# A projection stage rewritten: unrolled, with the vector work of one head pair laid behind the products of the next

## What is computed

```
def token_shift_mix(z, mu):
    prev = jnp.pad(z[:, :-1], ((0, 0), (1, 0), (0, 0)))
    nxt = jnp.pad(z[:, 1:], ((0, 0), (0, 1), (0, 0)))
    return z + mu * (0.5 * (prev + nxt) - z)

def rwkv_prepare(zs, w0, w2, a0, a2, g2, k_k, k_a):
    ...
    r, k, v, wd, ad, gd = [zs[..., bounds[i]:bounds[i + 1]] for i in range(6)]
    ...
    w_log = -jax.nn.softplus(-(w0 + jnp.einsum('btdl,dlc->btdc', jnp.tanh(wd), w2))) - 0.5
    decay = jnp.exp(-jnp.exp(w_log.astype(jnp.float32)))
    iclr = jax.nn.sigmoid(a0 + jnp.einsum('btdl,dlc->btdc', ad, a2))
    gate = jax.nn.sigmoid(gd) @ g2
    kk = split_heads(k * k_k).astype(jnp.float32)
    kk = kk * lax.rsqrt(jnp.maximum(jnp.sum(kk * kk, axis=-1, keepdims=True), L2_EPS * L2_EPS))
    k_dir = k[:, :, None, :] * (1.0 + (iclr - 1.0) * k_a)
```

## Time and profile before

| | |
|---|---|
| median of 3 runs | 2924.93 us (2923.62 to 2926.19) |
| the profiled execution, its own time | 2919.25 us |
| its span, first to last instruction | 2917.6 us |
| mean granted TensorE clock | 0.883 |
| busy in the span | TensorE 2215.9 us, VectorE 1730.8, ScalarE 859.6, GpSimd 721.5 |
| instructions | 41,994 |

### The profile page before, as it was taken

One profiled execution on the slowest core, in us unless ns is written; L12 is line 12 of the kernel. 1 busy time (PEld: TensorE's weight loads), 2 busy tenths in 40 slices (PEclk: granted clock), 3 DMA queues, 4 the chain that ended last, 5 costly groups with the idle time before them and its releaser, 6 DMA issues. The chain is left out here.

```text
span 2917.6 us, 41994 instructions
## 1 busy us (share of the span) xinstructions
PE 2215.9 (76%) x16681; PEld 1386.4 (48%) x16681; DVE 1730.8 (59%) x3472; ACT 859.6 (29%) x1718; POOL 721.5 (25%) x607
## 2 busy tenths in 40 slices
PE   5667667398767688887888898878777777777876
PEld 2645545187642677876665454333333332333332
DVE  2367767642582033433556666877777777777764
ACT  4244444232442323332332222222122212221221
POOL 0000000080000111111004333444444444444441
PEclk8888888699768699998999999999999999999898
DMA  3222322342523433230539999999999999999995
GB/s 159 69 88 86 148 109 86 143 150 81 225 99 124 176 140 133 90 140 17 187 128 399 363 384 342 421 411 420 421 420 420 421 421 420 420 421 421 421 421 220
DMA packets 119316, 741.36 MB, mean 254 GB/s; under 512 B 16065, under 2 KB 23265, under 8 KB 48353
## 3 DMA queue, kind: packets, MB, share of 16 engines
q0 software_dynamic: 73728, 536.90, 44.7%
q1 hardware_dynamic: 44256, 199.88, 18.5%
q10 hardware_dynamic: 1152, 2.10, 0.2%
HBM read 683.14 MB, written 55.69 MB: 253 GB/s over the span
## 5 line engine op out<-in xcount | busy, mean ns | idle before, releaser
L2278 PE MATMUL bank<-uv,dg 128*128 128x512 f32 x1664 | 810.4, 644 | 232.3 <-ACT dg L2086 227.4
L2278 PEld LDWEIGHTS bank<-uv,dg 128*128 128x128 f32 x1664 | 333.7, 205 | 699.6 <-issue 408.9
L2171 DVE SCALAR_TENSOR_TENSOR junk<-uv,gr 128x1024 f32<-128x1024 f32 x416 | 509.9, 1226 | 219.1 <-DMA uv<-in_uv_in,ic 193.3
L2009 POOL DMA_INDIRECT uv<-in_uv_in,ic x416 | 461.0, 1108 | 663.3 <-PE bank L2278 584.7
L2081 ACT ACTIVATE ge<-dt_ 128x4 f32<-128x4 f32 x128 | 26.5, 207 | 927.5 <-DVE junk L2171 927.4
L91 PE MATMUL bank<-ht_hi,wh 128*128 128x256 f32 (+1 forms) x432 | 164.4, 381 | 110.0 <-DVE wl L477 73.9
L2278 PE MATMUL bank<-uvx,dg 128*128 128x512 f32 x384 | 190.3, 653 | 56.5 <-ACT dg L2086 56.5
L2086 ACT ACTIVATE dg<-ident,gc_ 128x128 f32<-128x128 f32 x512 | 164.2, 392 | 29.4 <-DVE gc_ L2177 29.2
L91 PEld LDWEIGHTS bank<-ht_hi,wh 128*128 128x128 f32 x432 | 96.0, 222 | 136.3 <-issue 102.2
L92 PE MATMUL bank<-ht_lo,wh 128*128 128x256 f32 (+1 forms) x432 | 158.5, 367 | 0.0
L2278 PEld LDWEIGHTS bank<-uvx,dg 128*128 128x128 f32 x384 | 78.1, 209 | 168.7 <-issue 92.3
(11 more groups left out here) (357 smaller groups left out, 3982.9 us busy)
## 6 DMA issues: line engine op xcount, KB each, us to landing
pair_record<-rec SPq DMA_DIRECT2D x8, 4364.0 KB
wm<-in_wmod SPq DMA_DIRECT2D x16, 1024.0 KB, 5.1
wraw<-in_wpair_in SPq DMA_DIRECT2D x8, 1536.0 KB, 14.9
ab<-pair_record SPq DMA_DIRECT2D x16, 768.0 KB, 6.3
wz<-in_wz_in SPq DMA_DIRECT2D x20, 512.0 KB, 3.5
wm<-in_wmod SPq DMA_DIRECT2D x4, 2048.0 KB, 21.4
wraw<-in_wq_in SPq DMA_DIRECT2D x16, 512.0 KB
uv<-in_uv_in,ic POOLq DMA_INDIRECT x416
```

What stands on the lines that cost most here:

```text
L2009: pool.indirect_dma_start(ring(i), None, g["uv_in"], bass.IndirectOffsetOnAxis(ap=ic[:, s % ICR, k:k + 1], axis=0)).then_inc(su[row_slot[i ...
L2171: dve.scalar_tensor_tensor(junk[:, :], ring(i)[:, 0:D], 1.0, hc[:, t % 2, :], ALU.mult, ALU.mult, accum_out=dt[:, k:k + 1]).then_inc(s_ud, 1)
L2278: mm = pe.matmul(acc(t, c)[:, :], dg[:, n % 2, k, :], ring(i)[:, D + 512 * c:D + 512 * c + 512], start=h == 0 and q == 0 and k == 0, stop= ...
```

## The change

`project` is written again; its inputs, its output record and the amount of matmul work stay.

- All streams are written out; there is no loop, no `hold`, and semaphores count through.
- ScalarE makes only the scaled copy of a tile. VectorE adds mu/2 times each neighbour directly from the accumulators, in four instructions a tile (`shift`).
- Work of pair j-1 (unit kk, keys, queries, keys out, bonus, removal, addition) stands on VectorE between the shifts of pair j. `zs`, `al`, `kf` and `lw` have two buffers each; v goes to the record's field and not through `zs`.
- The reversed copies go; products of the second direction read their operands reversed (`parts`).
- The norm's inverse root is ScalarE's Ln and Exp(-x/2) in place of Sqrt and VectorE's reciprocal. The affine steps on decay and rate are ScalarE's; rates' 0.5 * (1 + x) is folded into two products.
- Weights are loaded tile by tile (512 KB) and the record is stored in seven fields.

```diff
-        zs = sb(st, "zs", [P, 3, T])
-        zr = sb(st, "zr", [P, 3, T])
+        zs = sb(st, "zs", [P, 2, 2, T])
+        al = sb(st, "al", [P, 2, NDIR, T])
+        kf = sb(st, "kf", [P, 2, NDIR, T])
...
+                for j in range(NPAIR + 1):
+                    if j + 1 < NPAIR:
+                        weights(3 * j + 8)
+                    if j:
+                        sp.wait_ge(s_r, 2 * j)
+                        stored("r", j - 1)
+                    if j < NPAIR:
+                        sp.wait_ge(s_gc, j + 1)
+                        stored("g", j)
+                    if j + 2 < NPAIR:
+                        weights(3 * j + 9)
+                    if j:
+                        sp.wait_ge(s_k, 2 * j)
+                        stored("k", j - 1)
+                        sp.wait_ge(s_bo, j)
+                        sp.wait_ge(s_ec, j)
+                        stored("o", j - 1)
+                    if j + 2 < NPAIR:
+                        weights(3 * j + 10)
...
-                    act.activation(rn[:, :], rn[:, :], ACT.Sqrt).then_inc(s_std, 1)
+                def rnorm(j):
+                    act.wait_ge(s_mx, 2 * j + 2)
+                    act.activation(rn[:, :], rn[:, :], ACT.Ln).then_inc(s_ln, 1)
+                    act.wait_ge(s_ln, j + 1)
+                    act.activation(rn[:, :], rn[:, :], ACT.Exp, scale=-0.5).then_inc(s_rn, 1)
...
+                for j in range(NPAIR):
+                    if j >= 2:
+                        act.wait_ge(s_b, 2 * (j - 1))
+                    scaled(3 * j + 3)
+                    high(3 * j + 5)
+                    if j:
+                        exps(j - 1)
+                    squared(j)
+                    decays(j)
+                    scaled(3 * j + 4)
+                    high(3 * j + 6)
+                    gate(j)
+                    rnorm(j)
+                    if j:
+                        act.wait_ge(s_bo, j)
+                        act.wait_ge(s_st["v"], 16 * j)
+                    scaled(3 * j + 5)
+                    high(3 * j + 7)
+                    rates(j)
+                    turned(j)
+                exps(NPAIR - 1)
...
-                def shift(q):
-
-                    for a, o, m in ((0, 0, CTX), (CTX, CTX + 2, SEQ)):
-                        ch(dve.tensor_tensor(ns[:, a:a + m], zp[:, q, o:o + m], zp[:, q, o + 2:o + 2 + m], ALU.add))
-                    ch(dve.scalar_tensor_tensor(zs[:, q, :], ns[:, :], col(HMU + q), zs[:, q, :], ALU.mult, ALU.add))
...
+                def shift(n):
+                    z, (half, _) = target(n), shift_cols(n)
+                    for i, ((a, m), b) in enumerate(zip(SEG, banks(n))):
+                        dve.wait_ge(s_zc, 2 * n + i + 1)
+                        dve.scalar_tensor_tensor(z[:, a + 1:a + m], b[:, 0:m - 1], half, z[:, a + 1:a + m], ALU.mult, ALU.add).then_inc(s_sh, 1)
...
+                def parts(d):
+                    return ((slice(0, NC), lambda a: chunks(a)),) if d == 0 else tuple(
+                        (slice(a // CHUNK, (a + m) // CHUNK), lambda t, a=a, m=m: chunks(t[:, a:a + m])[:, ::-1, ::-1]) for a, m in SEG)
...
+                def unit(j):
+                    dve.wait_ge(s_rn, j + 1)
+                    if j:
+                        dve.wait_ge(s_t, 3 * j)
+                    dve.scalar_tensor_tensor(uk[:, :], zs[:, j % 2, 1, :], col(j, KK), rn[:, :], ALU.mult, ALU.mult).then_inc(s_u, 1)
...
+                for j in range(NPAIR + 1):
+                    if j < NPAIR:
+                        shift(3 * j + 3)
+                        low(3 * j + 5)
+                    if j:
+                        unit(j - 1)
+                        keys(j - 1)
+                        queries(j - 1)
+                    if j < NPAIR:
+                        summed(j)
+                        shift(3 * j + 4)
+                        low(3 * j + 6)
+                        bounded(j)
+                    if j:
+                        keys_out(j - 1)
+                        bonus(j - 1)
+                    if j < NPAIR:
+                        shift(3 * j + 5)
+                        low(3 * j + 7)
+                    if j:
+                        removal(j - 1)
+                        addition(j - 1)
...
+                for j in range(NPAIR):
+                    product(3 * j + 3)
+                    pe.wait_ge(s_lw[j % 2], 16 * (j // 2) + 16)
...
+                    lora(j, 0, s_l0)
+                    product(3 * j + 4)
+                    pe.wait_ge(s_sq, j + 1)
+                    pe.wait_ge(s_lt, 4 * j + 4)
...
+                    if j:
+                        bonus(j - 1)
+                    product(3 * j + 5)
+                    pe.wait_ge(s_mx, 2 * j + 2)
+                    pe.wait_ge(s_gc, j + 1)
+                    if j:
+                        pe.wait_ge(s_bo, j)
+                    lora(j, 1, s_l1)
```

More of the change, by code:

```diff
@@ L355, in pair @@
[L355 to L367, removed]
@@ L374, in _ @@
+                for f in FIELDS:
+                    sp.wait_ge(s_st[f], 16 * NPAIR)
             @block.gpsimd
             def _(pool):
[L376 to L388, removed]
+                pool.memset(ex[:, :, :, 0:1], 1.0).then_inc(s_c, 1)
@@ new lines, in rates @@
+                def rates(j):
+                    act.wait_ge(s_l1, j + 1)
+                    for d in range(NDIR):
+                        for (a, m), b in zip(SEG, (bank[4 + 2 * d], bank[5 + 2 * d])):
+                            act.activation(al[:, j % 2, d, a:a + m], b[:, 0:m], ACT.Tanh, bias=col(j, HW + 2 + d),
+                                           scale=0.5).then_inc(s_at, 1)
+                    for d in range(NDIR):
+                        act.wait_ge(s_at, 4 * j + 2 * d + 2)
+                        act.activation(kf[:, j % 2, d, :], al[:, j % 2, d, :], ACT.Identity, bias=col(j, OKA),
+                                       scale=col(j, HKA)).then_inc(s_kf, 1)
@@ L464, in _ @@
-                with act.Fori(0, NPAIR - 1) as j:
-                    pair(j, False)
-                pair(NPAIR - 1, True)
+                act.wait_ge(s_vec, 1)
+                for n in range(3):
+                    scaled(n)
+                    high(n + 2)
+                act.wait_ge(s_zs, 3)
+                H, L = slice(64, P), slice(0, 64)
+                for i, f in ((0, ACT.Tanh), (1, ACT.Copy)):
+                    act.activation(lin[L, i, :], target(i)[L, :], f).then_inc(s_li, 1)
+                    for a, m in SEG:
+                        act.activation(lin[H, i, a:a + m], target(i)[H, a:a + m][:, ::-1], f).then_inc(s_li, 1)
@@ L658, in _, with bonus @@
-                with pe.Fori(0, NPAIR - 1) as j:
-                    pair(j, False)
-                pair(NPAIR - 1, True)
+                        for (a, m), b in zip(SEG, (bank[4 + 2 * d], bank[5 + 2 * d])):
+                            mm = pe.matmul(b[:, 0:m], lw[R, j % 2, i, :], lin[R, i, a:a + m], start=True, stop=True)
+                    mm.then_inc(done, 1)
+                def bonus(j):
+                    pe.wait_ge(s_bk, j + 1)
+                    pe.matmul(bank[7][:, :], blk[:, :], tb[:, :], start=True, stop=True).then_inc(s_bm, 1)
@@ L664, in gates @@
+                pe.wait_ge(s_at, 4 * NPAIR)
+                bonus(NPAIR - 1)
 def gates(nc, sb, sem, g):
```

458 lines of the change are left out of this document (229 added, 229 removed).

## The result

The changed kernel takes 2730.05 us (median of 4 runs, 2722.86 to 2733.78), the kernel before 2925.56 in the same comparison: ratio 0.9329, 95% interval 0.9307 to 0.9351, 195.5 us less. The forecast was 2752, range 2740 to 2786: the gain came out 13% larger than forecast, and the time lies under the range. The profiled execution took 2722.86 us, 196.4 less than that of before, where the forecast said 173.

The account below looks back on a forecast made before the run. A ring through VectorE was taken to bound each pair: 33.0 us plus 1.1 for semaphore changes, period 34.1. The next stage would start at 405.4, 173 us earlier, giving 2752 by the median; range 2740 to 2786.

Parts of the forecast that it names:

- VectorE's sum: VectorE's instructions for one pair in the projection, each its duration plus 0.03 us, summed to 32.3 us.
- changes of semaphore: VectorE's some 12 switches a pair to a semaphore raised by another engine, at 0.1 us each: 1.1 us.
- TensorE's list: TensorE's work for one pair: three products, low-rank groups, norm, gate and bonus, together 31.7 us at full clock.
- the ring: Dependent chain through VectorE, TensorE and ScalarE from one pair's norm bound to the next: 33.0 us, 34.1 with semaphore changes.
- rival 1: The ring as walked sets the pair's period, 33.0 to 35.5 us: kernel 2744 to 2762 us, chance 0.60.
- the drain: The last pair's vector work without shifts at the end of the projection stage: 16.6 us with changes.
- Rival 4: A better outcome, with drain or first load shorter and changes free: kernel 2735 to 2744 us, chance 0.05.
- The stage's frame: The projection stage between first load and next stage's first load: 505.2 us before, next stage starting 173 us earlier after.
- No table load between Ln and Exp: On ScalarE in the norm, Exp behind Ln needs no further table load: 0 taken, bounds 0 and 1.28 us a pair.
- ScalarE's term from the bound to Exp's end: On ScalarE, from the norm's bound through table load, Ln and Exp: 3.1 us before v's accumulator is scaled.
- Rival 2: The ring slips by a second table load, TensorE's lower clock or PSUM reads: period 35.5 to 38.5 us, chance 0.24.
- Rival 3: About 44 satisfied VectorE waits a pair cost 0.25 us more each, or a weight load sticks behind a store: chance 0.09.

Follow-up runs that it names:

- the run with gates: The changed kernel with gate increments put back on VectorE, every wait of its list followed by an increment of its own semaphore: stage 309.5 us, kernel 2726.2.
- the dear list: The changed kernel, skewed, with VectorE's reciprocal and its waits for the instruction before both put back: stage 381.0 us, period 41.0.

## Why the prediction was wrong

The failed step is VectorE's sum: "An instruction takes its duration plus 0.03 us to the next", 32.3 us, and 1.1 for changes of semaphore. Together, 33.4 us, they measured 28.55. The price came from a kernel in which nearly every VectorE instruction waits for the one before it, and was given to a list that mostly does not. Of the 4.85 us between, the run with those waits put back shows 4.3; the rest is the 1.1 for changes, of which the run with gates shows no trace, less roundings of the sum. The Trainium skill (VectorE: DVE Perf Modes, the section on two Vector instructions with no wait between them) says that an instruction which no rule holds starts before the earlier ones have finished; the trace agrees: 0.11 us each on average here.

The consequence was a wrong bound. With 28.55 on VectorE, TensorE's list is the longer, and that sum was right: 31.7 forecast, 31.40 measured. It stood in the text, and the ring had it as an arm with a slack of only 0.65, yet rival 1 took 33.0, VectorE's, as its least period. Seven periods at 2.7 less are 18.9 of the 22.9 us between 405.4 and 382.5; the drain was 14.2 and not 16.6 for the same reason. Rival 4, which had changes free and stopped at 2735, came nearest, with a chance of 0.05. The range was said to leave out 2 in 10; by its own chances it leaves out little more than 1.

By point:
- The stage's frame and that later stages do not change: right.
- Products at 8.34, first product from a third of the load, pair 0 bound by TensorE: right (high half at 77.07 against 77.3, third product's end at 106.6 against 106.4).
- Reading accumulators and reversed reads at no extra cost: right, 0.746 for 511 and the reversed 512 at 0.69. The shift out of the accumulators was priced 1.1 us dearer a pair (7.8 against 6.7); VectorE's list shows 0.1.
- No table load between Ln and Exp: wrong, 1.28 us in every pair (L482). It cost nothing in this kernel, as the third product ends later. ScalarE's term from the bound to Exp's end was right by luck, 3.1 us forecast and 3.05 measured (194.67 to 197.72): it had a load on the way before Ln, which was hidden, and none before Exp, where one stands. Of the set with both functions, which the Trainium skill names (ScalarE: Activation LUTs, Table sets), the trace shows no use: there are both loads, and the one before Ln is issued ahead of its wait (189.75, with Ln at 194.71).
- Weights and stores hidden: right with seven fields, and not with four in one.
- Rival 2 (clock and a ring that slips) did not occur; its price for the clock, 1.7 us, measured 1.5 in the run with the reciprocal, in every second pair. Rival 3 (waits at 0.25 more each) is refuted by VectorE's list, and by the run with gates.

What the 23.2 us of a pair consist of, taken in one order: 3.0 skew (31.4 to 34.4), 7.8 the reciprocal and the waits for the instruction before (34.4 to 42.2, unskewed). In the other order they are 9.6 and 1.2. The last 12.4 (42.2 to 54.56) weren't taken apart: affine passes and copies on VectorE, the loop, single buffers, and the norm's product behind the third tile (6.6 us of wait a pair) are all in them.

## What to carry to other kernels

When a list of instructions is costed for a new order, take the pitch of two that stand in the same relation as they will, waiting or not waiting for each other; where a kernel is chained nearly throughout, look for the few places that are not, as the two low halves here. Put the lower end of a range at the sum of the next engine, not at the least of the engine believed to bind. And where TensorE is close to full, look for what frees the accumulator that its next product writes: moving that one instruction opens a ring which filling a visible stall leaves shut. Then look at the other engines' periods too: a TensorE that never waits may only be using up a lead that another engine has over it.

## What the runs showed that was not expected

- A wait for an instruction just issued on the same engine costs 0.11 us on average on VectorE, 4.3 us over 40 instructions; a wait for another engine's semaphore that is already there, with an increment after it, costs nothing that shows: 0.2 us over the whole list, at the one place where the wait is for VectorE itself.
- After an idle stretch of TensorE the granted clock fell in some pairs and not in others, so the length of the wait alone does not decide it. Behind 2.35 us the group took 1.57 us in some pairs and 2.06 in another (clock 1.00 and 0.73, the run with the reciprocal); behind 2.55 it took 1.57 or 2.94 (clock 1.00 and 0.50, the run with every instruction waiting); behind 4.21 it took 2.94 each time (0.50, the dear list).
- The table for Exp was loaded again straight behind Ln, 1.28 us, though the load before Ln was issued ahead of the wait and so was hidden.
- With TensorE's work cut, the next bound was a loop of VectorE and ScalarE alone, 30.1 us in two runs, through Ln, the table load and Exp.
